# Two reorderings in a two-layer encoder kernel: input-matrix transposes ahead of a projection run in the even layer's attention, and one bank read ahead of two splits in the odd layer's value projection

## What is computed

```python
# layer 0 (even)
qa, ka, va, ub = split(h @ even_w_in)          # 512 columns each
oa = chunk_band_attention(qa, ka, va, rel)     # softmax, 8 heads of 64
ob = s5_mixer(ub, ...)                         # 32 groups of 16 channels, 64 complex states each
mix = concatenate([oa, ob]) @ even_w_out
# layer 1 (odd)
qc, kc, vc = split(h @ odd_w_in)               # 1024 columns each
mix = stick_breaking_attention(qc, kc, vc) @ odd_w_out
```

## Time and profile before

| | before |
|---|---|
| median of three runs | 1151.65 us (1151.4 to 1152.92) |
| the profiled execution | 1152.04 us, of which the span of the records is 1150.2 us |
| granted TensorE clock, mean | 0.998 |
| PE busy | 1128.6 us, 98% of the span |
| DVE busy | 888.0 us, 77% |
| POOL busy | 558.9 us, 49% |
| ACT busy | 551.2 us, 48% |

### The profile page before, as it was taken

How to read it: one execution, slowest core, us unless ns; L and a number is a source line. 1 busy time by engine, 2 the same in 40 slices (tenths; PEclk the granted TensorE clock), 3 DMA queues, 4 the chain that set the end, 5 groups by cost and what they waited for, 6 DMA issues and landing times.

```text
span 1150.2 us, 19245 instructions
## 1 busy us (share of the span) xinstructions
PE 1128.6 (98%) x7437; PEld 983.3 (85%) x7437; DVE 888.0 (77%) x1234; ACT 551.2 (48%) x864; POOL 558.9 (49%) x360
## 2 busy tenths in 40 slices
PE   7999999999999999999999999999999999999997
PEld 6877668899999999888887777777999999998886
DVE  8558653887888888995965787766987888889947
ACT  6435565245444554453455555533445444544540
POOL 5898614356577764013795222203576676760000
PEclk9999999999999999999999999999999999999999
DMA  7623325143334335226144121202523333352331
GB/s 213 184 78 88 106 76 201 37 129 111 94 103 116 93 111 178 97 92 219 45 124 125 56 66 45 74 1 74 143 79 110 111 111 93 110 160 98 98 122 74
DMA packets 161754, 122.04 MB, mean 106 GB/s; under 512 B 19408, under 2 KB 140280, under 8 KB 161664
## 3 DMA queue, kind: packets, MB, share of 16 engines
q1 hardware_dynamic: 161664, 120.82, 35.1%
HBM read 117.37 MB, written 3.43 MB: 105 GB/s over the span
## 4 chain that ended last, share of the span: by engine, by line
PE 91%; DVE 4%; POOL 2%; ACT 1%; DMA 1%; issue 1%; SPq 1%; DVEq 0%; ACTq 0%; POOLq 0%
PE ps L2320 18%; PE ps L2322 17%; PE ps L2321 17%; PE ps L2350 6%; PE ps L2352 6%; PE ps L2351 6%; PE ps L2343 4%; PE ps L2345 4%; PE ps L2344 4%; PE ps L2881 2%; PE ps L2907 2%; PE ps L2892 2%; POOL wlo L926 1%; PE ps L2357 1%; PE ps L2925 1%; DMA h<-in_x 1%
## 5 line engine op out<-in xcount | busy, mean ns | idle before, releaser
L926 POOL TENSOR_TENSOR wlo<-raw,whi 128x1024 fp32r<-128x1024 f32 x73 | 178.2, 2455 | 253.6 <-ACT whi L1081 245.5
L2320 PE MATMUL ps<-xhi,whi 128*128 128x256 f32 (+1 forms) x848 | 272.1, 321 | 0.0
L2322 PE MATMUL ps<-xhi,wlo 128*128 128x256 f32 (+1 forms) x848 | 267.0, 315 | 0.0
L2321 PE MATMUL ps<-xlo,whi 128*128 128x256 f32 (+1 forms) x848 | 266.8, 315 | 0.0
L2320 PEld LDWEIGHTS ps<-xhi,whi 128*128 128x128 f32 x848 | 161.7, 191 | 17.7 <-issue 6.4
L1005 POOL TENSOR_TENSOR wlo<-raw,whi 128x512 fp32r<-128x512 f32 x114 | 173.2, 1545 | 0.6 <-ACT whi L1371 0.5
L2320 PE MATMUL ps<-thi,whi 128*128 128x256 f32 x608 | 172.2, 283 | 0.0
L2321 PE MATMUL ps<-tlo,whi 128*128 128x256 f32 x608 | 172.2, 283 | 0.0
L2322 PE MATMUL ps<-thi,wlo 128*128 128x256 f32 x608 | 172.2, 283 | 0.0
L2322 PEld LDWEIGHTS ps<-xhi,wlo 128*128 128x128 f32 x848 | 161.8, 191 | 10.4
L2321 PEld LDWEIGHTS ps<-xlo,whi 128*128 128x128 f32 x848 | 161.9, 191 | 8.4
(11 more groups left out here) (324 smaller groups left out, 2482.6 us busy)
## 6 DMA issues: line engine op xcount, KB each, us to landing
raw<-in_ffn_w SPq DMA_DIRECT2D x126, 512.0 KB, 3.9
raw<-in_odd_w_in SPq DMA_DIRECT2D x22, 512.0 KB, 3.8
raw<-in_even_w_in SPq DMA_DIRECT2D x16, 512.0 KB, 4.5
t<-in_ffn_w SPq DMA_DIRECT2D x12, 512.0 KB, 6.6
h<-in_x SPq DMA_DIRECT2D x8, 512.0 KB, 5.2
raw<-in_even_w_out SPq DMA_DIRECT2D x8, 512.0 KB, 3.6
raw<-in_odd_w_out SPq DMA_DIRECT2D x8, 512.0 KB, 3.5
bias<-rel_scratch SPq DMA_DIRECT2D x8, 256.0 KB, 3.7
```

What stands on the lines that cost most here:

```text
L926: eng.tensor_tensor(lo, source_of(b), hi, ALU.subtract).then_inc(w_lo, 1)
L2320: eng.matmul(o_, w_hi_, x_hi_, start=start, stop=False)
L2321: eng.matmul(o_, w_hi_, x_lo_, start=False, stop=False)
L2322: return eng.matmul(o_, w_lo_, x_hi_, start=False, stop=stop)
```

## The change

The first part moves parts 0 and 1 of quarter 2 on two engines, in step n = 2 alone: on PE ahead of the projection run, on ACT ahead of the exponentials of piece 3. The second part splits a loop over two row tiles on DVE, so that the first bank of P7 is read before the two splits of `s_lower(P3)` and the second one behind them.

```diff
+        STATES_FIRST = (2,)
...
             for n in range(-1, A_PIECES):
+                if n in STATES_FIRST:
+                    ssm_outs(SSM_BEFORE[n])
                 if n + 1 < A_PIECES and n not in QK_FIRST:
                     softmax_exp(n + 1)
...
-                ssm_outs(SSM_BEFORE.get(n, ()))
+                if n not in STATES_FIRST:
+                    ssm_outs(SSM_BEFORE.get(n, ()))
...
+            v_add(v_of(0, 1), sg[:, 0, :], P7, 0, ALU.subtract)
             s_lower(P3)
-            for t in range(2):
-                v_add(v_of(t, 1), sg[:, t, :], P7, t, ALU.subtract)
+            v_add(v_of(1, 1), sg[:, 1, :], P7, 1, ALU.subtract)
...
                 if n + 1 < A_PIECES:
                     scores(n + 1)
+                if n in STATES_FIRST:
+                    ssm_products(SSM_BEFORE[n])
                 if runs:
                     aqk(*runs[0])
-                ssm_products(SSM_BEFORE.get(n, ()))
+                if n not in STATES_FIRST:
+                    ssm_products(SSM_BEFORE.get(n, ()))
```

## The result

The changed kernel took **1157.64 us** as the median of five runs (1157.23 to 1157.73) against 1152.88 us for the kernel before on the same chip (1151.4 to 1154.08): ratio 1.0045, 95% interval 1.0034 to 1.0056. It is slower by 4.8 us, where the prediction had 0.55 us less than before and a range that ended at 1153.0 us. The profiled execution has a span of 1155.8 us.

A forecast was written before the change was run, and what follows sets the result against it. The prediction took PE, busy for 98% of the span, as the bound. Its terms, -0.55 us for the first part and 0 for the second, summed to -0.55 us: from 1151.65 to 1151.1 us, range 1149.5 to 1153.0 us.

The forecast's parts named there:

- The gain of 1.68 us at part 2: Part 2 of the third quarter on PE: no wait for ACT's copy `wini`, start 1.68 us sooner, the whole gain on offer.
- (a): PE's scores of piece 4 wait for piece 3's biases, 2.8 us later; 0.9 us of the 1.68 us lead is left.
- (b): `toep` of the second quarter lands at 112.3 us, PE wants it at 113.0 us: no stall, 0.7 us to spare.
- (c): PE's projection 5 waits for `qT`, ending at 115.4 us with 1.2 us for the multiplies; lead left 0.55 us.
- the 10.6 us: Span on ACT in the kernel before, from the start of piece 3's exponentials to `qT`; the forecast took 1.45 us off.
- rival 4: Slower: piece 3's multiplies fall behind POOL's operations (2.66 us), PE 0.9 us behind at projection 5, 1152.6 us; chance 0.13.
- (d): Third quarter's `toep` at 131.97 us: POOL's chain keeps at least 0.55 us, stall stays about 0.7 us, then only PE counts.
- The clock: Transfers or clock levels changing elsewhere could make the forecast wrong at large; the rows of before show none hanging here.
- Part 2: DVE's earlier read of P7's first bank: P6 still waits for POOL's lower part at about 587.8 us, gain 0 us.
- Rival 3: Nothing left: `build_out(3, 0)` loses its lead at DVE's products, PE waits 1.3 us for `toep`, 1151.65 us; chance 0.15.
- rival 5: Something not seen moves the kernel's time by more than 2.3 us either way; chance 0.05.

The follow-up runs named there:

- e11: e6 with POOL's first hold released sooner, by DVE's add `gk` instead of the biases of piece 3: 1149.64 us, ratio 0.9976 to the kernel before.
- e7: Changed kernel with only POOL's `build_out(3, 0)` held until `xsr` and `xsi` of the third quarter are written: 1153.99 us, ratio 1.0014 to the kernel before.
- e5: Changed kernel with `build_in(3)` held until piece 3's biases and `build_out(3, 0)` until the third quarter's `xsr` and `xsi`: 1151.39 us, ratio 0.9992 to before.
- e6: e5 with POOL's split for block 15 moved ahead of the second hold and `build_out(3, 0)`: 1148.62 us, ratio 0.9974 to the kernel before.
- e8: Changed kernel, same orders and waits, POOL's operations from the fourth quarter's input to output matrices and two splits cut to 16 elements or fewer: 1148.63 us, ratio 0.9971.
- e9: Changed kernel with `build_in(3)` held, `build_out(3, 0)` free and block 15's split held until `xsr` and `xsi`: 1150.73 us, ratio 0.9979 to the kernel before.
- e1: Changed kernel with POOL's `build_in(3)` held until DVE has added the biases of piece 3: 1155.40 us, ratio 1.0028 to the kernel before.
- e4: Changed kernel with ACT's copies back behind the exponentials, PE's transposes still early: 1155.75 us, ratio 1.0031 to the kernel before.
- e3: Changed kernel without the early transposes and copies, keeping only DVE's split reads of P7: 1151.92 us, ratio 1.0001 to the kernel before.
- e2: Changed kernel with the reads of P7 as before, keeping only the early transposes and copies: 1158.07 us, ratio 1.0049 to the kernel before.
- e10: e6 without the early transposes and copies on PE and ACT, keeping POOL's new order and holds: 1151.77 us, ratio 0.9993 to the kernel before.

## Why the prediction was wrong

**Right, nearly all with their sizes.** The gain of 1.68 us at part 2 is there. POOL's `build_in(3)` starts at 101.69 us, which is 100.75 us with 0.94 us off, the predicted time. `xsr`, `xsi` and `gk` take 1.17, 1.28 and 1.25 us (predicted 1.1 to 1.3, and about 1 for `gk`), the exponentials of piece 3 start at 106.2 us (107.11 less 0.91; predicted 106.25), and (a) costs PE 0.69 us (predicted 0.8). The rule that the prediction drew on, the Trainium skill's page "SBUF — State Buffer", section "SBUF: two separate sides", which has the shared port pair as a lock for a whole instruction, is borne out by these rows, and by e11 from the other side: an operation with one input in PSUM is not held. (b) was right for `toep`, but PE waits 0.40 us there for `zin_i`, which the prediction did not have.

**(c), a term off in size.** The prediction gave the pair of multiplies of piece 3 1.2 us, because POOL's "next split waits for a cast that ACT makes only at 108.5 to 109.5 us". It doesn't: the split starts at 109.04 us, straight behind `wni` and before ACT's cast of 109.31 us, so it needed an earlier one: step 1 of ACT's queue makes the cast for this block, that of 109.31 us is for the block behind it. The pair took 3.01 us. The rest of the 10.6 us held: from the exponentials to the end of `qT` it is 10.98 us, 1.83 us over the predicted 9.15, and the pair is 1.81 us of it. The profile names nobody for PE's wait ahead of projection 5 (`issue`), but `qT` ends at 118.09 us, 0.1 us ahead of its end. PE waited 1.64 us there instead of 0.3 and started it at 117.3 us (118.19 less 0.91), 1.2 us behind the kernel before instead of 0.55 us ahead. This is rival 4, a little beyond its price.

**(d), the step that failed.** "POOL's chain keeps at least the 0.55 us", and behind it "nothing but PE sets the time until the end of the stage". It looked only at what POOL's chain delivers to SP and not at what it meets. In the kernel before, POOL is released at 116.22 us when DVE has been in its multiplies and products since 114.85 us, and DVE is through them before the split of 121.65 us. Now POOL is released at 116.65 us, and DVE, late from (c), begins its multiplies only at 117.86 us: nearly every instruction of that row meets POOL, one of them the split. The biases of piece 5 come 6.7 us later (127.29 less 0.91, against 119.65), ACT's exponentials, and behind them `yT`, with them, and PE waits 3.27 us. e7 takes only this second meeting away and the wait is gone; e5, e6, e8 and e9 do it together with the first, and it is gone in all. DVE's lateness from (c) is not needed for it: in e1, where (c) costs nothing, POOL comes 0.14 us behind the start of DVE's multiplies (116.38 and 116.24 us), and the wait is 3.32 us long. The mechanism was the one that the prediction had priced some 16 us earlier in the same queue; it was not followed to the next place where the same two engines meet. Together with (c), in the table of cuts: 2.14 us at the places of (b) and (c), 3.89 us at that of (d), against 0.96 and 0.38 us won.

**The clock.** The prediction held that no row of before hung on it. After the 3.27 us wait PE's rows run at 0.51, and the stretch of 1.65 us takes 3.05 us, 1.4 us more. The cuts give the same, as the difference to a version without either: 14.97 - 10.28 - 3.27 = 1.4 us in the changed kernel, 15.13 - 10.28 - 3.32 = 1.5 us in e1, and 1.5 us in e4 at its own place. No experiment changed the clock alone, so this is an account of rows and not a separate proof.

**Part 2.** Predicted 0, found 0.4 to 0.6 us. The profile names POOL's `wlo` as what ended the wait, and the prediction took it as what P6 needed. It was only the last to end, 0.1 us behind DVE's read of the first bank (587.81 and 587.71 us); e3 starts P6 before the same split is over.

**The rivals.** Rival 4 had the right mechanism at the first place with a chance of 0.13 and 0.9 us; its price ended at projection 5. Rival 3 saw that `build_out(3, 0)` "meets DVE's products at another phase", but let the cost fall on POOL where it fell on DVE. The slow side of the range was therefore 4.6 us too near. By its size the result is rival 5, a move of more than 2.3 us by something not seen, which had a chance of 0.05 for both directions together.

**Open.** In the kernel before, DVE's row of products kept POOL waiting (1.60 us for a 0.6 us operation); in e9 the same two queues take turns from 115.12 us on. The traces sort by where POOL comes in: in the changed kernel, e1, e2 and e9 it is there before or during DVE's four multiplies, and the two take turns; in before and e3 it comes 1.4 us behind the start of the multiplies, when DVE is in its products, and waits. What decides between the two was not isolated.

## What to carry to other kernels

An instruction moved ahead on a busy engine is also a release for somebody: list whose waits it ends, and follow that engine's queue to every later place where its operations can hold up the engine that the critical copies hang on, not only to the first. Such a move can be kept and its side effect taken back by letting the released engine wait for a point where the other has time to spare: here two holds and one exchange in POOL's queue turned +4.7 us into -3.1 us by the cuts (+4.8 and -3.6 us by the medians). Of these 3.1 us, 1.2 us come without the move (e10). A releaser in the profile is the last event, not the needed one; where two end within 0.1 us, price both.

## What the runs showed of the hardware

- An add of 16 elements that takes 0.17 us alone took 1.25 us, and a product of 256 elements 2.62 us instead of 0.42, each ending just behind one operation of POOL. What such an instruction cost in these rows followed POOL's operation, not its own size.
- A scan with both inputs in SBUF is held in the same way: the second one took 0.66 us in e1 and 2.81 us beside a split in e6. So are the multiplies by the row sums, which have only one large input: 0.89 us for the pair alone and 3.01 us here, 1.14 us for four and 2.38 us here.
- After waits of 3.27 us (after) and 4.44 us (e4) PE's next rows were at a granted clock of 0.51 and 0.57 over the window, near its 1.2 GHz level, and cost some 1.5 us more; after 3.32 us in e1 it was 0.56, and as much was lost; after a wait of 1.68 us (9.05 us from piece 2 to 3 in e10, 7.30 us without the wait in e6) nothing was lost but the wait itself.
